# Last attention of a two-block network: scores of the first key group by query quarters, softmax steps between value tiles, weighting moved into the next chunk

## What is computed

```python
WINDOWS = (128, 512, 2048)
DILATIONS = (1, 4, 16)
def dilated_branch(q, k, v, window, dil):
    # Query t attends keys t - j*dil, j = 0..window//dil.
    ...
    scores = jnp.einsum("brhnqc,brhnkc->brhnqk", q_blk, k_band) * (1.0 / math.sqrt(dh))
    scores = jnp.where(valid, scores, NEG_INF)
    m = jnp.max(scores, axis=-1, keepdims=True)
    p = jnp.exp(scores - m)
    den = jnp.sum(p, axis=-1, keepdims=True)
    out = jnp.einsum("brhnqk,brhnkc->brhnqc", p, v_band) / den
    return out, m + jnp.log(den)

def dilated_mixture_attention(h, w_q, w_o, k, v):
    q = (h @ w_q).reshape(b, s, N_GROUPS, N_HEADS, HEAD_DIM_2)
    ... # one dilated_branch for each group
    merged = jnp.sum(softmax(lses)[..., None] * outs, axis=0)
    return merged.reshape(b, s, N_HEADS * HEAD_DIM_2) @ w_o
```

## Time and profile before

| | us |
|---|---|
| median of 3 runs | 3195.36 (3194.01 to 3195.73) |
| profiled execution | 3197.16 |
| its span, first to last instruction | 3195.4 |
| PE busy | 3105.5 |
| DVE busy | 1874.6 |
| ACT busy | 1279.6 |

### The profile page before, as it was taken

How to read it: one execution, slowest core, us unless ns; L and a number is a source line. 1 busy time by engine, 2 the same in 40 slices (tenths; PEclk the granted TensorE clock), 3 DMA queues, 4 the chain that set the end, 5 groups by cost and what they waited for, 6 DMA issues and landing times.

```text
span 3195.4 us, 42324 instructions
## 1 busy us (share of the span) xinstructions
PE 3105.5 (97%) x16855; PEld 2565.3 (80%) x16855; DVE 1874.6 (59%) x2534; ACT 1279.6 (40%) x1780; POOL 181.4 (6%) x231
## 2 busy tenths in 40 slices
PE   7999999999999999999999999999999999999999
PEld 7767888888877788888887578888878888788887
DVE  3574456657656544555777866567553443555666
ACT  3562234336444522433562343346331222343355
POOL 2030000000013000000001200000000000000000
PEclk9999999999999999999999899999999999999999
DMA  6207843235512476323452179235576121222244
GB/s 175 64 27 230 202 121 106 92 101 166 144 57 77 144 200 170 106 92 104 131 165 67 54 228 220 98 109 174 195 190 147 64 92 54 80 86 92 95 132 161
DMA packets 290266, 400.49 MB, mean 125 GB/s; under 512 B 19556, under 2 KB 202892, under 8 KB 289868
## 3 DMA queue, kind: packets, MB, share of 16 engines
q1 hardware_dynamic: 242588, 298.36, 28.8%
q0 software_dynamic: 47536, 100.14, 13.2%
HBM read 396.28 MB, written 85.98 MB: 151 GB/s over the span
## 4 chain that ended last, share of the span: by engine, by line
PE 85%; DVE 9%; ACT 3%; DMA 2%; issue 1%; DVEq 0%; ACTq 0%; SPq 0%; POOL 0%; POOLq 0%
PE ps L1889 19%; PE ps L1890 19%; PE ps L1891 19%; PE ps L2050 4%; PE ps L2051 4%; PE ps L2052 4%; DVE t_wlo L1232 2%; PE ps L2002 1%; PE ps L1928 1%; PE ps L1926 1%; PE ps L2004 1%; PE ps L1927 1%; PE ps L2003 1%; DMA t_wraw<-in_w_in_dram 1%; ACT t_whi L791 1%
## 5 line engine op out<-in xcount | busy, mean ns | idle before, releaser
L1232 DVE TENSOR_TENSOR t_wlo<-t_wraw,t_whi 128x2048 fp32r<-128x2048 f32 x198 | 461.0, 2328 | 991.9 <-ACT t_whi L791 991.9
L1889 PE MATMUL ps<-t_hh,t_whi 128*128 128x512 f32 (+1 forms) x2704 | 1015.2, 375 | 21.1 <-DVE t_hl L1329 8.2
L1891 PE MATMUL ps<-t_hh,t_wlo 128*128 128x512 f32 (+1 forms) x2704 | 1004.6, 372 | 0.0
L1890 PE MATMUL ps<-t_hl,t_whi 128*128 128x512 f32 (+1 forms) x2704 | 1004.6, 372 | 0.0
L791 ACT ACTIVATE t_whi<-t_wraw 128x2048 fp32r<-128x2048 f32 x198 | 379.3, 1916 | 1113.5 <-PE ps L1891 850.9
L1889 PEld LDWEIGHTS ps<-t_hh,t_whi 128*128 128x128 f32 x2704 | 513.1, 190 | 126.7 <-issue 25.2
L1890 PEld LDWEIGHTS ps<-t_hl,t_whi 128*128 128x128 f32 x2704 | 513.1, 190 | 87.7 <-issue 2.4
L1891 PEld LDWEIGHTS ps<-t_hh,t_wlo 128*128 128x128 f32 x2704 | 512.6, 190 | 87.4
L2050 PE MATMUL ps<-t_whi,t_ah 128*128 128x512 f32 x528 | 206.0, 390 | 0.0
L2051 PE MATMUL ps<-t_wlo,t_ah 128*128 128x512 f32 x528 | 205.5, 389 | 0.0
L2052 PE MATMUL ps<-t_whi,t_al 128*128 128x512 f32 x528 | 205.4, 389 | 0.0
(11 more groups left out here) (316 smaller groups left out, 4253.4 us busy)
## 6 DMA issues: line engine op xcount, KB each, us to landing
t_wraw<-in_w_in_dram SPq DMA_DIRECT2D x46, 1024.0 KB, 6.2
t_wraw<-in_w_up_dram SPq DMA_DIRECT2D x44, 1024.0 KB, 5.1
t_wraw<-in_ffn_w_in_dram SPq DMA_DIRECT2D x44, 1024.0 KB, 5.1
t_wraw<-sum_T SPq DMA_DIRECT2D x80, 512.0 KB, 4.0
sum_T<-in_w_down_dram POOLq DMA_DIRECT2D x12, 2560.0 KB, 32.6
sum_T<-in_ffn_w_out_dram POOLq DMA_DIRECT2D x12, 2560.0 KB, 29.9
t_wraw<-in_w_kv_dram SPq DMA_DIRECT2D x24, 1024.0 KB, 5.2
sum_T<-sum_T POOLq DMA_DIRECT2D x8, 2560.0 KB, 19.0
```

What stands on the lines that cost most here:

```text
L1232: v.tensor_tensor(wlo[slot][:, :], wraw[slot][:, :], whi[slot][:, :].bitcast(F32), ALU.subtract).then_inc(w_lo, 1)
L1889: te.matmul(out, wh, xh, start=first, stop=False)
L1890: te.matmul(out, wh, xl, start=False, stop=False)
L1891: return te.matmul(out, wl, xh, start=False, stop=last)
```

## The change

- **Tokens in natural order.** `hh`, `hl` are no longer permuted. Queries still are (`hq`). Keys of groups 1 and 2 are brought to residue order when DVE copies them out of PSUM (`drain`), keys of group 0 stay in token order. For the values of groups 1 and 2 the stationary operand is read with a step of four elements (`d_tokens`).
- **Group 0 by query quarters.** A block of 128 queries of one residue is cut into four quarters of 32. The tokens of a quarter lie within 128, so 256 keys do. Its scores are a matmul with 32 stationary columns and 256 keys; the four write to partitions 0, 32, 64 and 96 of one bank.
- **Fewer scores.** A step has 512 scores in place of 768. Queries are scaled by a negative factor, so that one DVE instruction adds the mask and takes the minimum (`minimum`). ACT takes the exponent from PSUM. Four pieces are turned, not six.
- **Order of chunks.** Keys, then queries, then values. One step's turns (`D_TURNS`) and another's scores (`D_SCORES`) stand ahead of each value token tile but the first and the last.
- **Weighting.** The turned probabilities of a whole pair are kept, in `gain` and in tiles of `yD`. A head is weighted at once (`d_weigh`): 8 matmuls for groups 1 and 2 and 7 for group 0, each with 128 columns. The two heads' weightings stand after the two row tiles of the next pair's first chunk, for the last pair between the two halves of `out3`.
- **Split of the output.** The split of `yD` for the output product is spread over the last pair (`mixed_hi`, `mixed_lo`).
- Masks come with one transfer in place of two; copies stand ahead of `lo` on DVE.

```diff
-            dmask = sb("dmask", 7 * P, stack=s)
-            near = gain[:, 3 * T:3 * T + 2 * P]
+            pD = sb("pD", SLOTS * T, stack=s)
+            dmask = sb("dmask", 10 * P, stack=s)
...
-        D_ORDER = [[(kD, 0), (vD, 0), (kD, 1), (vD, 1), (kD, 2), (qD, 0), (qD, 1), (qD, 2), (vD, 2)]]
-        D_ORDER += 3 * [[(kD, 0), (vD, 0), (qD, 0), (kD, 1), (vD, 1), (qD, 1), (kD, 2), (qD, 2), (vD, 2)]]
+        D_ORDER = [(buf, g) for buf in (kD, qD, vD) for g in range(3)]
+        D_SCORES, D_TURNS = range(1, 9), range(3, 11)
...
+            def exp(hp, n):
+                ...
+                sc.activation(pD[:, p * T:(p + 1) * T], bank(4 + n % 2), ACT.Exp, bias=small[:, q:q + 1], scale=-1.0,
+                              accum_out=small[:, 8 + q:9 + q]).then_inc(probs, 1)
...
+                for n in range(10):
+                    if n >= 2:
+                        copy(hp, n - 2)
+                    if n < 8:
+                        exp(hp, n)
+                    if hp == 3 and n in (0, 2):
+                        mixed_hi(n, n + 2)
+                    if n in (3, 7):
+                        hi(c + 9 * hp + (6 if n == 3 else 7))
...
+            def drain(hp, i):
+                dve.wait_ge(w_used, c + 9 * hp + i + 1)
+                dst, g = D_ORDER[i]
+                ...
+                    elif dst is qD:
+                        ins = v.tensor_scalar(tile(dst, 2 * g + h), bank(b), -SD, None, ALU.mult)
+                    elif g:
+                        ins = v.tensor_copy(by4(tile(dst, 2 * g + h)), permuted(bank(b)))
...
+            def minimum(hp, n):
+                ...
+                v.tensor_tensor_reduce(scores, scores, masks, 1.0, -2 * NEG, ALU.add, ALU.min,
+                                       small[:, q:q + 1]).then_inc(maxed, 1)
...
+                for n in range(8):
+                    minimum(hp, n)
+                    divide(STEPS["D"] + 8 * hp + n, pD, T)
+                    if hp == 3 and n in (0, 2):
+                        mixed_lo(n, n + 2)
+                    if n in (3, 7):
+                        drain(hp, 6 if n == 3 else 7)
+                        lo(c + 9 * hp + (6 if n == 3 else 7))
...
+            def d_tokens(u, k, g, b):
+                return u[:, k * T + b:(k + 1) * T:4] if g else u[:, k * T + b * P:k * T + (b + 1) * P]
...
+                for r in range(4):
+                    keys = tile(kD, m).rearrange("p (r n) -> p r n", r=4)
+                    keys = keys[:, r - 1:r + 1] if r else keys[:, 0:1].broadcast_to([P, 2, P])
+                    te.matmul(halves(bk[32 * r:32 * r + 32, WIN:2 * WIN]), at(qD, 0, 32 * r, 32 * r + 32), keys, start=True, stop=True)
+                for g in (1, 2):
+                    ins = te.matmul(bk[:, (g - 1) * P:g * P], at(qD, g), at(kD, g), start=True, stop=True)
...
+                for b in range(4):
+                    for g in (1, 2):
+                        te.matmul(out[:, b * P:(b + 1) * P], values(b, g), d_turned(hp, m, b)[:, (g - 1) * P:g * P], ...)
+                every = d_turned(hp, m, 0, 4).rearrange("p (b k l) -> p k b l", b=4, k=4)
+                for r in range(4):
+                    for back in ((1, 0) if r else (0,)):
+                        ins = te.matmul(out.rearrange("p (b l) -> p b l", b=4)[:, :, 32 * r:32 * r + 32], values(r - back, 0),
+                                        every[:, 3 - back, :, 32 * r:32 * r + 32], ...)
...
             for hp in range(4):
+                for i in range(0 if hp else 3, 6):
+                    d_rows(hp, i, [lambda hp=hp, m=m: d_weigh(hp - 1, m) for m in range(2)] if hp and i == 0 else (None, None))
+                for s in range(12):
+                    i, b = divmod(s, 4)
+                    if b == 0:
+                        start(c + 9 * hp + 6 + i, d=d + 9 * hp + 6 + i)
+                    if s in D_TURNS:
+                        d_turn(hp, D_TURNS.index(s))
+                    if s in D_SCORES:
+                        d_scores(hp, D_SCORES.index(s))
+                    ins = d_values(hp, 6 + i, b)
...
-            pe.wait_ge(h_lo, SPLIT["y"] + 1)
-            out_product(3, (qh, ql), "y", None)
+            pe.wait_ge(pt_ready, STEPS["D"] + 32)
+            out_product(3, (qh, ql), "y", None, last_weigh)
```

More of the change, by code:

```diff
@@ L141, in host_constants @@
     l, m = np.arange(P)[:, None], np.arange(P)[None]
[L142 to L145, removed]
+    steps = [np.where(l >= m, 0, -NEG), np.where((l >= m) & ((l - m) % 4 == 0), 0, -NEG)]
+    key = np.arange(2 * P)[None]
+    for b in range(4):
+        back = P + 4 * (l % 32) + b - key
+        steps.append(np.where((back >= 0) & (back <= P) & ((l >= 32) | (key >= P)), 0, -NEG))
+    dmask = np.concatenate(steps, axis=1).astype(np.float32)
     return {"c_base": np.concatenate([ident, head, mean, rot, np.roll(ident, 64, axis=1)], axis=1), "c_rope": np.concatenate([cos, sin], axis=1),
@@ L1211, in _ @@
                         row_hi("hq", qh, 2 * j + 1, 3)
[L1212 to L1215, removed]
+                for n in range(10):
[7 more added lines that the diff above has]
+                        hi(c + 9 * hp + (6 if n == 3 else 7))
+                if hp == 3:
+                    mixed_hi(4, 6)
+                hi(c + 9 * hp + 8)
+            mixed_hi(6, 8)
             out_rows(3)
@@ new lines, in head_out, with mixed_lo @@
+            def head_out(hp, m):
+                dve.wait_ge(weighted, STEPS["D"] + 8 * hp + 4 * m + 4)
+                v.tensor_copy(tile(yD, 2 * hp + m), d_mix_bank(hp, m)).then_inc(y_lo, 1)
+            def mixed_lo(t0, t1):
+                for t in range(t0, t1):
+                    dve.wait_ge(h_hi, SPLIT["y"] + t + 1)
+                    v.tensor_tensor(permuted(tile(ql, t)), by4(tile(yD, t)), permuted(tile(qh, t).bitcast(F32)),
+                                    ALU.subtract).then_inc(h_lo, 1)
@@ L1851, in _ @@
+            scale_row("hq", 0)
+            scale_row("hq", 1)
+            for hp in range(4):
+                for i in range(6):
+                    if hp and i == 0:
+                        head_out(hp - 1, 0)
+                    drain(hp, i)
+                    lo(c + 9 * hp + i)
+                    if hp and i == 0:
+                        head_out(hp - 1, 1)
                     if hp == 0 and i < 2:
@@ L1856, in _ @@
                             scale_row("hq", 3)
[L1857 to L1878, removed]
+                if hp == 0:
+                    dve.wait_ge(tables, 16 * 10)
+                for n in range(8):
[6 more added lines that the diff above has]
+                        lo(c + 9 * hp + (6 if n == 3 else 7))
+                if hp == 3:
+                    mixed_lo(4, 6)
+                drain(hp, 8)
+                lo(c + 9 * hp + 8)
+            for m in range(2):
+                head_out(3, m)
+                mixed_lo(6 + m, 7 + m)
             out_rows(3)
@@ L2061, in out_product @@
                     tokens_mix(c + j, 0, bufs, 4 * j, 4 * j + 4, KT - 1, lambda k: (h_lo, SPLIT[split] + k + 1))
+                    if between and j == 0:
+                        between()
                 if banks_free:
```

276 lines of the change are left out of this document (116 added, 160 removed).

## The result

| | before | after |
|---|---|---|
| median (runs beside each other) | 3195.55 (3194.01 to 3196.98, 4 runs) | 3231.05 (3228.76 to 3232.11, 4 runs) |
| profiled execution, its span | 3197.16, 3195.4 | 3231.20, 3229.4 |
| PE busy | 3105.5 | 3161.0 |

The ratio is 1.011 (95%: 1.0093 to 1.0128). The forecast of 3143 was wrong, and the range too. The time is that of case 2, 3223 to 3235.

A forecast was written before the change was run, and what follows sets the result against it. PE's stream was taken as the bound, with DVE setting the pace in attention steps. 3197.2 - 26.4 (stream) - 28.0 (gaps) + 2 (hand-overs) = 3144.8, less 1.8 for the median: 3143 us; range 3135 to 3184.

The forecast's parts named there:

- case 2: Rival: strided stationary loads of value chunks cost in full, 80 to 92 us more, 3223 to 3235; chance 0.20.
- the term for the strided stationary operand: Value chunks of groups 1 and 2: 768 matmuls load with a step of 16 bytes; taken as 0 us extra.
- the upper bounds of 80 and 92: Strided value loads: 768 x 0.105 = 80 us more at most, or 92 if the distance doubles.
- the 2 that I had left for hand-overs: PE's attention stretch: some 2 us of gaps expected to remain in hand-overs, a chosen figure between nothing and 8.
- The gaps: PE gaps from pair one's first scores to the end of out3's first chunk: 28.0 us, to go but for 2.
- PE's stream: Scores, turns and weighting on PE: 19.8 us a pair where it had 26.4, so 26.4 us less over four pairs.
- case 5: Rival: group 0's four quarter score matmuls run one after another, 32 steps x 1.28 = 41 us more, 3184; chance 0.04.
- case 4: Rival: softmax results reach PE late, at two places a pair or every step; 3150 to 3165 us; chance 0.07.
- The point of decision: Strided value loads: an extra cost from 52/768 = 0.068 us for each matmul on decides whether the change is slower.

The follow-up runs named there:

- the doubled group: The repaired kernel (tokens permuted, group 0's values made as row tiles and turned) with each group of four quarter score matmuls issued twice: 3156.1 us.
- Step 3: The changed kernel with the stationary operand of groups 1 and 2's value chunks read every three elements (12 bytes) instead of four, on other tokens: 3186.43 us.

## Why the prediction was wrong

- **The step that failed** is the term for the strided stationary operand, put at nothing: "I take 0: the slow rows are writes, and DVE's one strided read there shows no cost beyond that of ACT, which only writes so". That read is the one of `qh` in L1877, `v.tensor_tensor(permuted(tile(ql, t)), by4(tile(yD, t)), permuted(tile(qh, t).bitcast(F32)), ALU.subtract)`. It is a read of SBUF with the step in question, but it stands in one instruction with a write of the same step. If it costs as much as that write it does not show, so the row gave no reason for 0. What the row did price, 0.105 us for 128 elements, was the right size: measured are 0.114 a load, 87.5 us in all, between the upper bounds of 80 and 92. I chose the other end, and left 0.20 for this one.
- **The sum with the measured load** is 3197.2 - 26.4 - 28.0 + 768 x 0.114 (87.5) = 3230.3, without the 2 that I had left for hand-overs; the profiled execution took 3231.2.
- **The gaps** (28.0 us, of which 2 to stay): PE has no wait left in the stretch and the clock stays at 1.00. With loads in a row the median is 3141.7 against 3143 forecast.
- **PE's stream** (26.4 us less): right as a sum, 119.8 for 119.6 a pair, and partly by luck. In a slot three sizes were off and cancel: quarters 0.57 for 0.77, turns 0.53 for 0.43, and the scores of groups 1 and 2 with the slower first product behind them 0.46 + 0.09 = 0.55 for 0.44. Weighting was sized right, 3.35 us a head. The changed kernel, between the halves of `out3`:

```profile
2831.32 1.95 PE L2508 MATMUL ps<-t_gain,t_vD 128*128 128x128 f32 x16
2833.10 1.73 PE L2513 MATMUL ps<-t_gain,t_vD 128*128 128x128 f32 x14
2834.67 1.95 PE L2508 MATMUL ps<-t_yD,t_vD 128*128 128x128 f32 x16
```

Group 0's runs of 32 columns (L2513) cost 1.57 / 7 = 0.224 each, as much as 128 columns in a row (1.78 / 8).

- **Quarters in series** (case 5): refuted by the doubled group. **Late softmax** (case 4): absent. With loads in a row PE waits once, 0.3 us, from 2300 to 2800. The minimum, read of its result included, takes 0.84 for my 0.9:

```profile
L1850 DVE DVE_READ_ACCUMULATOR2_ANT t_small<- x32: 133/142/148, 2332.9 to 2797.9; 128x1 f32 x32
L1850 DVE CUSTOM_DVE_ANT_1 ps<-ps,t_dmask x24: 685/700/700, 2334.5 to 2797.3; 128x512 f32<-128x512 f32 x24
```

- **The point of decision** was named: from 0.068 us a matmul on, the loads eat the gain. Step 3, with 0.054, stays below it (3186.43, against 3192.39 to 3201.03 of the kernel before beside it); step 4 does not.

Open is why the write costs in the earlier trace rows match the load's; two hits a line would explain both, but no run varied the step of a write, or a read of DVE without one. Nor did a run read with uneven steps, which would tell a price by touched pieces from one by the step itself.

## What to carry to other kernels

Keep the stationary operand of a matmul at a step of 8 bytes or less in SBUF, and the moving one off a step of 16 (8 was not tried there). Reorder where it is free: in the copy out of PSUM. When a form of access has no row of its own, a row where it stands beside something slower does not show that it is free; a neighbour with a price is the better guide. Attention steps between tiles of independent products hid the softmax chain here, and their cost on PE could then be summed from matmul spacings.

## What the runs showed of the hardware that was not expected

- A load of 128 fp32 columns costs by the 16-byte pieces that it touches: steps 1 and 2 hide under 0.12 us, 3 takes 0.174, and 4 and 8, with the same number of pieces, take 0.233 and 0.240.
- The moving operand pays as well: 512 columns with step 4 take 0.46 for 0.227.
- DVE reads PSUM with a step of 16 bytes as fast as in a row (686 ns for 512 elements, and 686).
- A weight load that is always busy (20.00 of 20 us) need not be the bound: it is so at 192 ns and at 329 ns a load.
- A group of four matmuls with 32 stationary and 256 moving columns costs 0.43 us inside and 0.14 at its edges.
